# Three of five RMS-norms: four chunks' squares summed as the moving operand in four column tiles, the rest with one output column

## The chip, the cores and the metric

The kernel runs on one core of one Trainium2 chip. The metric is the device time of one execution in microseconds (us); the kernel before was run three times, and its time is the median of them.

## The reference, cut to what matters

A two-layer backbone works on a stream x of 256 tokens by 1024 channels. Each layer has a mixer (layer 0: attention beside a pooling mixer; layer 1: a Fourier mixer) and a channel mixer (layer 0: a dense SwiGLU; layer 1: a top-2-of-8 expert SwiGLU). An RMS-norm with a modulation stands ahead of each of the four, and a last norm behind them:

```python
def rmsnorm(x, g):
    x32 = x.astype(jnp.float32)
    y = x32 * lax.rsqrt(jnp.mean(x32 * x32, axis=-1, keepdims=True) + EPS)
    return (y * g.astype(jnp.float32)).astype(x.dtype)

for i in range(DEPTH):                      # DEPTH = 2
    h = modulate(x, norm_mix_g[i], sh1, sc1)    # rmsnorm(x, g) * (1 + scale) + shift
    mix_l = attention_and_pool(h) if i == 0 else fourier_mix(h)
    x = x + g1 * mix_l
    h = modulate(x, norm_ffn_g[i], sh2, sc2)
    x = x + g2 * (swiglu(h) if i == 0 else moe_swiglu(h))
return rmsnorm(x, final_g)
```

Everything is float32. What matters here is the mean of x*x over the 1024 channels of each token.

## The kernel before, in words

The stream lies transposed in SBUF: `x` is 8 chunks (KD = 8) of 128 channels by 256 tokens (T = 256). The channels of a chunk are the partitions, so a mean over channels is a sum over partitions, which TensorE does. The norms have stage numbers: 0 ahead of attention, 1 ahead of the dense SwiGLU, 2 ahead of the Fourier mixer, 3 ahead of the experts, 4 at the end. The change touches 1, 2 and 3.

The engines run in parallel, each through its own program in order; semaphores (`wait_ge`, `then_inc`) order them against one another. There is no planner: the order is written out by hand. A norm of stages 1 to 3 goes so:

- TensorE finishes output chunks in PSUM (by pairs of chunks, one bank each).
- VectorE adds each to the stream (`add_projected`, L1077; count `residual`), a chunk at a time.
- ScalarE squares each chunk of the new stream into `square_l` (`squares`, L835; count `squared`).
- TensorE averages (`mean`, L1554): for each chunk k and each half t of the tokens the squares are the *stationary* operand, 128 x 128, and a constant 128 x 128 block with 1/1024 everywhere (`C("mean")`) is the moving one. A float32 product is two pairs of instructions (LDWEIGHTS and MATMUL), so a chunk is 4 pairs and a norm 32. Every one of the 128 output columns holds the same mean; `per_token` reads column 0 of each half.
- ScalarE takes the root of 128 x 2 values (`root`, L711), VectorE the reciprocal (L1011), TensorE spreads it over the partitions (`spread_root`, L1563), and VectorE scales the stream with it.

Where `mean` stands in TensorE's order differs:

- Stage 1 (`project`, "mixout", bank 6): the last piece of the output projection is done in two halves of columns. Behind the first half (which releases residual chunks 4 and 5) stand the means of chunks 0 to 3, then the second half of columns (12 products, L1592), then chunks 4 to 7. VectorE, ahead of adding chunk 4, splits the first dense weight piece (`dense_low(0)`, L1025).
- Stage 2 (bank 2): the last dense piece goes by four pairs of output chunks (L1808, 12 products each). The means of chunks 0 and 1 stand behind pair 2 (the third), those of 2 and 3 behind pair 3 (the last), then those of 4 to 7. Behind them stand the first four products of `shift_logits` (L1849) and then `spread_root`.
- Stage 3 (`project`, "fnet", bank 0): as stage 1, but the means of 4 and 5 are followed by the first half of the router (L1895: four column tiles, the partitions 0, 32, 64 and 96 on, of a weight with 8 columns, 256 moving columns), those of 6 and 7 by its second half. Then ScalarE copies the logits (L900), TensorE turns them (L1903), VectorE picks the experts (from L1309), TensorE ranks (L1917) and gathers (L1934), and the experts begin (L1964).

`C("fold")` is a constant whose column 0 has a 1 in the partitions 0, 32, 64 and 96 and 0 elsewhere; before, it adds up the router's four tiles and those of `shift_products`. `rstd` is an SBUF tile that is unused while stages 1 to 3 run. Semaphores `cq_taken`, `kv_taken` and `shift_rows_taken` belong to the latent projections of the attention (L1137 to L1166).

Of the kernel before, what the change touches and what calls it, by code (L numbers as in the profile page):

```python
# [12 lines left out]
ACT = mybir.ActivationFunctionType  # L13
AX_X = mybir.AxisListType.X

P = 128
D = 1024
KD = D // P
T = 256
# [19 lines left out]
QUAD = 32  # L39
# [85 lines left out]
SUM_GROUPS = ((0, 2), (2, 6), (6, 10), (10, 14))  # L125
# [62 lines left out]
def build(nc, vec_d, con_d, rope_d, x_d, ctx_d, ada_d, mixa_d, mixb_d, attn_d, mixout_d, ffn_d,  # L188
          dft_d, fnet_d, router_d, moe_d, out_d):
    ctx = ExitStack()  # L190
    with ctx:
# [3 lines left out]
        def sem(name):  # L195
            return ctx.enter_context(nc.semaphore(name))
# [36 lines left out]
        def C(name):  # L233
            return con[:, CON[name][0]:CON[name][1]]
# [71 lines left out]
        def plain(ap):  # L306
# [16 lines left out]
        squared, half_squared, mean_ready, root_ready = sem("squared"), sem("half_squared"), sem("mean_ready"), sem("root_ready")  # L323
        shift_rows, shift_rows_taken, shift_ready, shift_taken, kr_gained = (
            sem("shift_rows"), sem("shift_rows_taken"), sem("shift_ready"), sem("shift_taken"), sem("kr_gained"))
        token_ready, rstd_spread = sem("token_ready"), sem("rstd_spread")
# [5 lines left out]
        mixa_ready, mixa_taken = sem("mixa_ready"), sem("mixa_taken")  # L332
        cq_taken, kv_taken = sem("cq_taken"), sem("kv_taken")
        lora_squared, lora_mean, lora_root, lora_ready = (
# [162 lines left out]
        def prep_taken(eng, n):  # L497

            s = prep_act if PREP_BY[n] == "act" else prep_dve
            eng.wait_ge(s, sum(b == PREP_BY[n] for b in PREP_BY[:n + 1]))  # L500

        PART_BANKS = (5, 6, 7, 3)
        TOK_ORDER, TOK_BANKS = (0, 2, 1, 3), (1, 3, 2, 0)
# [177 lines left out]
        def _(act):  # L681
# [78 lines left out]
            mixer_highs("mixin", 6, 8)  # L760
            act.wait_ge(shift_taken, 1)
            act.wait_ge(mixer_used, 8)
# [68 lines left out]

            def squares(need):
                for k in range(KD):
                    act.wait_ge(residual, need + k + 1)
                    nc.scalar.activation(square_l[:, k, :], x[:, k, :], ACT.Square).then_inc(squared, 1)  # L835


            nc.scalar.activation(small[:, 242:243], C("eps"), ACT.Sqrt)
            squares(0)
            root(1, per_token(6), token_root)  # L840
# [26 lines left out]
            nc.scalar.activation(small[:, 242:243], C("eps"), ACT.Sqrt)  # L867
            squares(KD)
            root(2, per_token(2), token_root)
# [18 lines left out]

            squares(2 * KD)
            root(3, per_token(0), token_root)  # L890
# [66 lines left out]
        def _(dve):  # L957
# [178 lines left out]
            dve.wait_ge(shift_rows, 1)  # L1136
            nc.vector.tensor_copy(ada_rows[:, 0:416], bank[6][:, 0:416]).then_inc(shift_rows_taken, 1)  # L1137
            dve.wait_ge(shift_ready, 1)
            nc.vector.tensor_copy(mix_shift, bank[7][:, 0:8]).then_inc(shift_taken, 1)

            dve.wait_ge(shift_taken, 1)
            dve.wait_ge(mixer_used, 8)
# [6 lines left out]
            for k in range(2):  # L1149
                ins = shifted(cqT[:, k, :], bank[3][:, k * T:(k + 1) * T], 2 * k)  # L1150
            ins.then_inc(cq_taken, 1)
            for n in range(2):
                ins = shifted(ckvT[:, n * T:(n + 1) * T], bank[4][:, n * T:(n + 1) * T], 4 + n)
            ins.then_inc(kv_taken, 1)
            dve.wait_ge(kr_ready, 1)
            dve.sem_inc(unit_free[unit_slot(first_unit["mixb"])], 1)
            for n in range(2):
                ins = shifted(krT[:, n * T:(n + 1) * T], bank[5][:, n * T:(n + 1) * T], 6 + n)
            ins.then_inc(kv_taken, 1)
            dve.wait_ge(cq_taken, 1)  # L1160
            dve.wait_ge(kv_taken, 2)
            dve.wait_ge(lora_root, 2)
# [335 lines left out]
        def _(pe):  # L1498
# [50 lines left out]
            def mean(stage, before, source, b, lo=0, hi=KD):  # L1549
# [6 lines left out]
                if hi == KD:  # L1556
                    last.then_inc(mean_ready, 1)

            def spread_root(stage, b):

                pe.wait_ge(token_ready, stage)
                for t in range(2):
                    last = mm(bank[b][:, T + t * P:T + (t + 1) * P], token_root[:, t:t + 1].to_broadcast([P, P]), C("ident"),  # L1563
                              start=(t == 0), stop=(t == 1), skip_group_check=True)
                last.then_inc(rstd_spread, 1)

            def project(name, source, banks, stage, before, b):

                for m in range(first_piece[name], first_piece[name] + len(MIXER[name])):
# [15 lines left out]
                    for columns in ((0, 1), (2, 3)) if closing else ((0, 1, 2, 3),):  # L1585
                        for left, right in PRODUCTS:
                            if left == 1:
                                pe.wait_ge(mixer_low, m + 1)
                            for j in columns:
                                c = 4 * n + j  # L1590
                                for k in range(2):
                                    last = mm(bank[banks[c // 2]][:, (c % 2) * T:(c % 2) * T + T],  # L1592
                                              parts[left][:, k, j * P:(j + 1) * P], source[right][:, k0 + k, :],
                                              start=((left, right) == PRODUCTS[0] and k0 + k == 0 and c % 2 == 0),
                                              stop=((left, right) == PRODUCTS[-1] and k0 + k == KD - 1), skip_group_check=True)
                        if closing and columns[0] == 0:
                            last.then_inc(proj_ready, 1)
                            if n == 1:
                                mean(stage, before, square_l, b, 0, 4)
                    last.then_inc(mixer_used, 1)  # L1600
                if name == "mixout":
                    mean(stage, before, square_l, b, 4)

# [57 lines left out]
            def turn_shift():  # L1661

                pe.wait_ge(shift_rows_taken, 1)
                for n in range(4):
                    last = mm(bank[7][:, 2 * n:2 * n + 2], ada_rows[:, n * P:(n + 1) * P], C("fold")[:, 0:2], start=True, stop=True)
                last.then_inc(shift_ready, 1)
# [36 lines left out]
            pe.wait_ge(attn_in, 2 * 16)  # L1703
            pe.wait_ge(kv_taken, 2)
            for n, (kind, p) in enumerate(PREP):
# [86 lines left out]
            for q, (kind, g) in enumerate(DENSE):  # L1792
# [8 lines left out]
                if q == len(DENSE) - 1:  # L1801
                    pe.wait_ge(low_ready, q + 1)
                    for pair in range(4):
# [7 lines left out]
                        last.then_inc(ffn_ready, 1)  # L1811
                        if pair >= 2:
                            mean(2, 2 + KD, square_l, 2, 2 * (pair - 2), 2 * (pair - 1))
                    continue
# [24 lines left out]
                if q in (6, 14, 22, 30):  # L1839
                    sum_up((q - 6) // 8)  # L1840
            mean(2, 2 + KD, square_l, 2, 4)
            pe.wait_ge(router_in, 16)
# [45 lines left out]
            project("fnet", fourier, FNET_BANKS, 3, 2 + 2 * KD, 0)  # L1888
            mean(3, 2 + 2 * KD, square_l, 0, 4, 6)
            for half in range(2):  # L1890
                if half == 1:
                    mean(3, 2 + 2 * KD, square_l, 0, 6)
                pe.wait_ge(h_ready, KD + 4 * half + 4)
                for c in range(4):
                    last = mm(bank[4][c * QUAD:c * QUAD + EXPERTS, 0:T], router[:, 4 * half + c, :], h[:, 4 * half + c, :],  # L1895
                              start=(half == 0), stop=(half == 1), skip_group_check=True)
# [208 lines left out]
```

## Time and profile before

| | us |
|---|---|
| median of 3 runs | 1332.42 |
| lowest and highest of them | 1331.06, 1336.16 |
| the profiled execution, its own time | 1333.01 |
| its span in the trace | 1331.1 |
| what lies around the span | 1.9 |

Mean granted TensorE clock over the profiled span: 0.997 of full speed. The time of a part is read from the starts of the instructions around it: the engine's weight loads (PEld) and products (PE) are listed apart, and a group "x16" gives the first start and the length up to the last end. An idle time in brackets stands with the engine or transfer that ended it.

### The profile page before, as it was taken

What the parts mean: (1) busy time and instruction counts of PE and PEld (TensorE: products, weight loads), DVE (VectorE), ACT (ScalarE), POOL (GpSimd) and SP (SyncE); (2) the same over time, 40 slices, a digit from 0 to 9 for tenths busy, and PEclk for the clock granted to TensorE, in tenths of its full rate; (3) what the DMA queues carried; (4) which work ended last, traced back from release to release, by engine and by line L of the source; (5) the groups of instructions that cost most, each with busy time, mean ns of one, the idle gap of its engine ahead of it and who ended that gap; (6) DMA issues with size and microseconds to landing.
All of it is one profiled execution on the core that took longest, in us unless ns stands there. A gap on an engine that the chain in (4) does not pass through costs nothing.

```text
span 1331.1 us, 28323 instructions
## 1 busy us (share of the span) xinstructions
PE 1303.4 (98%) x12611; PEld 678.6 (51%) x12611; DVE 424.2 (32%) x829; ACT 234.7 (18%) x400; POOL 16.8 (1%) x34
## 2 busy tenths in 40 slices
PE   8988999999999999999999999999999999999997
PEld 7755899999997333333333333433333333333333
DVE  5537589999765001110020020111003002011103
ACT  5156534434353000000000000010000000000002
POOL 0400000000000000000000000000000000000000
PEclk9989999999999999999999999999999999999999
DMA  9773288998735789999999999999799999999980
GB/s 381 311 299 145 96 319 344 373 367 334 288 146 203 283 359 377 409 421 360 411 420 386 406 422 395 387 399 421 309 412 420 376 404 422 421 371 411 420 361 33
DMA packets 60693, 459.97 MB, mean 346 GB/s; under 512 B 6944, under 2 KB 7200, under 8 KB 9120
## 3 DMA queue, kind: packets, MB, share of 16 engines
q1 hardware_dynamic: 60576, 458.18, 85.1%
q8 instruction: 101, 1.65, 0.5%
q14 instruction: 16, 0.13, 0.0%
HBM read 457.04 MB, written 1.11 MB: 344 GB/s over the span
## 4 chain that ended last, share of the span: by engine, by line
PE 83%; DVE 10%; DMA 4%; issue 2%; ACT 1%; SPq 0%; DVEq 0%; PEldq 0%; ACTq 0%
PE bank L1964 43%; PE bank L1977 22%; DVE work L1040 5%; DMA ring<-in_ada 4%; PE bank L1592 3%; DVE split L1025 3%; PE bank L1641 2%; PE bank L1514 2%; PE bank L1944 1%; PE bank L1554 1%; PE bank L1934 1%; PE bank L1883 1%; PE bank L1833 1%; PE bank L1766 1%; DMA ring<-in_ctx 1%
## 5 line engine op out<-in xcount | busy, mean ns | idle before, releaser
L1964 PE MATMUL bank<-ring,work 128*32 128x512 f32 (+1 forms) x6144 | 584.9, 539 | 1.1 <-DVE moe L1449 1.1
L1964 PEld LDWEIGHTS bank<-ring,work 128*32 128x32 f32 x6144 | 199.3, 110 | 377.2 <-issue 344.1
L1977 PE MATMUL bank<-ring,moe 128*32 128x512 f32 x2688 | 294.1, 592 | 0.0
L1449 DVE TENSOR_TENSOR moe<-moe,bank 128x256 f32<-128x256 f32 (+1 forms) x96 | 31.5, 383 | 658.5 <-ACT moe L929 658.5
L1977 PEld LDWEIGHTS bank<-ring,moe 128*32 128x32 f32 x2688 | 87.4, 110 | 197.6 <-issue 196.2
L929 ACT ACTIVATE moe<-bank 128x256 f32<-128x256 f32 (+1 forms) x96 | 27.4, 358 | 792.3 <-PE bank L1964 792.3
L1833 PE MATMUL bank<-split 128*128 128x256 f32 x1056 | 131.0, 284 | 1.4 <-DVE split L1025 1.2
L1833 PEld LDWEIGHTS bank<-split 128*128 128x128 f32 x1056 | 128.0, 192 | 3.5 <-DVE split L1025 1.7
L1025 DVE TENSOR_TENSOR split<-ring,split 128x2048 fp32r<-128x2048 f32 x33 | 75.5, 2290 | 11.3 <-PE bank L1592 5.9
L1040 DVE SCALAR_TENSOR_TENSOR work<-ring,condp,work 128x512 f32<-128x512 f32 x98 | 73.7, 752 | 6.3 <-DMA ring<-in_ada 2.5
L852 ACT ACTIVATE split<-ring 128x2048 fp32r<-128x2048 f32 x32 | 61.2, 1914 | 81.7 <-PE bank L1833 73.7
L1823 PE MATMUL bank<-split 128*128 128x256 f32 x480 | 59.5, 284 | 0.0
L1823 PEld LDWEIGHTS bank<-split 128*128 128x128 f32 x480 | 58.3, 192 | 0.4 <-issue 0.4
L1592 PE MATMUL bank<-split 128*128 128x256 f32 x384 | 47.2, 284 | 0.0
L1592 PEld LDWEIGHTS bank<-split 128*128 128x128 f32 x384 | 46.4, 192 | 0.4 <-issue 0.4
L1435 DVE SCALAR_TENSOR_TENSOR xT<-bank,ada,xT 128x256 f32<-128x256 f32 x64 | 25.9, 477 | 62.1 <-PE bank L1944 62.1
L973 DVE TENSOR_TENSOR split<-ring,split 128x1024 fp32r<-128x1024 f32 (+1 forms) x24 | 28.1, 1179 | 13.4 <-ACT split L702 13.3
L1453 DVE STREAM_TRANSPOSE moe<-moe 128x256 f32<-128x256 f32 (+1 forms) x96 | 31.7, 381 | 0.0
L702 ACT ACTIVATE split<-ring 128x1024 fp32r<-128x1024 f32 (+1 forms) x24 | 24.2, 1018 | 24.2 <-PE bank L1592 18.4
L1641 PE MATMUL bank<-split 128*128 128x256 f32 x168 | 24.6, 303 | 1.3 <-PE bank L1514 1.3
L1514 PE MATMUL bank<-ring,condp 128*32 128x128 f32 x640 | 21.2, 289 | 4.5 <-DMA ring<-in_ada 4.3
L1641 PEld LDWEIGHTS bank<-split 128*128 128x128 f32 x168 | 21.4, 191 | 3.5 <-issue 3.0
(233 smaller groups left out, 634.0 us busy)
## 6 DMA issues: line engine op xcount, KB each, us to landing
ring<-in_moe SPq DMA_DIRECT2D x336, 1024.0 KB, 13.5
ring<-in_ffn SPq DMA_DIRECT2D x16, 2048.0 KB, 8.8
ring<-in_ada SPq DMA_DIRECT2D x28, 1024.0 KB, 7.2
ring<-in_ada SPq DMA_DIRECT2D x10, 2048.0 KB, 10.7
ring<-in_mixout SPq DMA_DIRECT2D x2, 2048.0 KB, 10.0
ring<-in_fnet SPq DMA_DIRECT2D x2, 2048.0 KB, 9.2
ring<-in_mixa SPq DMA_DIRECT2D x2, 1024.0 KB, 17.5
tail<-tables SPq DMA_DIRECT2D x8, 256.0 KB, 17.7
```

What stands on the lines that cost most here:

```text
L852: nc.scalar.activation(high_d[:, q % SPLITS_DENSE, :], piece_view(q), ACT.Copy).then_inc(high_ready, 1)
L1025: nc.vector.tensor_tensor(low_d[:, q % SPLITS_DENSE, :], piece_view(q), plain(high_d[:, q % SPLITS_DENSE, :]), ALU.subtract).then_inc(low_ ...
L1040: ins = nc.vector.scalar_tensor_tensor(out=total, in0=half_view(h)[:, k, :], scalar=weight, in1=total, op0=ALU.mult, op1=ALU.add)
L1449: nc.vector.tensor_tensor(gate_e[:, g, 0:n], gate_e[:, g, 0:n], bank[g][:, n:2 * n], ALU.mult).then_inc(e_hidden, 1)
L1453: nc.vector.transpose(hiddenT[phase % 2][:, g, 0:n], gate_e[:, g, 0:n]).then_inc(e_turned, 1)
L1514: last = mm(bank[RUNS[run][2]][32 * j:32 * j + 32, u * P:(u + 1) * P], cond[:, k, :], w[:, k, j * P:(j + 1) * P], start=(k == 0), stop=(k ...
L1592: last = mm(bank[banks[c // 2]][:, (c % 2) * T:(c % 2) * T + T], parts[left][:, k, j * P:(j + 1) * P], source[right][:, k0 + k, :], start= ...
L1641: last = mm(out, parts[left][:, k, lo:hi], h_in[right][:, k0 + k, 0:n], start=((left, right) == PRODUCTS[0] and k0 + k == 0 and opens), st ...
L1823: last = mm(bank[FFN_BANKS[k // 2]][:, (k % 2) * T:(k % 2) * T + T], w[:, j, k * P:(k + 1) * P], hidden_parts[g % 2][:, right, j, :], star ...
L1833: last = mm(bank[kind == "w3"][:, j * T:(j + 1) * T], w[:, k, j * P:(j + 1) * P], h_parts[:, right, k, :], start=(n == 0 and j == 0 and k ...
L1964: last = mm(bank[g][c * QUAD:(c + 1) * QUAD, 0:count * P], x_group[:, 4 * half + k, j * CAP + g * QUAD:j * CAP + (g + 1) * QUAD], source[: ...
L1977: last = mm(bank[3 + n][c * QUAD:(c + 1) * QUAD, :], hiddenT[phase % 2][:, g, blk * QUAD:(blk + 1) * QUAD], source[:, j, n * 512:(n + 1) * ...
```

## The change

The means of chunks 0 to 3 become `quarters`: the constant, 32 columns of it, is the stationary operand and the squares are the moving one (256 tokens); chunk c goes to column tile c, that is, partitions 32c to 32c+31 of a bank of its own (7, 3 and 1 for stages 1, 2 and 3). ScalarE copies that bank to `rstd` between the squares of chunk 3 and of chunk 4. `mean_rest` then turns the copy to one column for each half of the tokens with `C("fold")[:, 0:1]` as moving operand, and adds the means of chunks 4 to 7 with *one* moving column in place of 128. In stage 2 all of `quarters` stands behind the last pair. Stages 0 and 4 keep theirs. Three semaphores are merged with others: `shift_rows_taken` into `shift_taken` (counts 1 and 2), `cq_taken` and `kv_taken` into `lora_taken` (3).

```diff
+        QUARTER_BANKS = (None, 7, 3, 1)
@@ ScalarE
-            def squares(need):
+            def squares(need, stage=None):
                 for k in range(KD):
+                    if stage and k == 4:
+                        act.wait_ge(quarters_ready, stage)
+                        nc.scalar.activation(rstd[:, 0:T], bank[QUARTER_BANKS[stage]][:, 0:T], ACT.Copy).then_inc(quarters_taken, 1)
                     act.wait_ge(residual, need + k + 1)
                     nc.scalar.activation(square_l[:, k, :], x[:, k, :], ACT.Square).then_inc(squared, 1)
...
-            squares(0)
+            squares(0, 1)
...
-            squares(KD)
+            squares(KD, 2)
...
-            squares(2 * KD)
+            squares(2 * KD, 3)
@@ the merged semaphores: ScalarE and VectorE, then TensorE
-            act.wait_ge(shift_taken, 1)
+            act.wait_ge(shift_taken, 2)
...
-            dve.wait_ge(cq_taken, 1)
-            dve.wait_ge(kv_taken, 2)
+            dve.wait_ge(lora_taken, 3)
...
-            pe.wait_ge(kv_taken, 2)
+            pe.wait_ge(lora_taken, 3)
@@ TensorE
+            def quarters(stage, before):
+
+                pe.wait_ge(squared, before + 4)
+                for c in range(4):
+                    last = mm(bank[QUARTER_BANKS[stage]][c * QUAD:(c + 1) * QUAD, 0:T], C("mean")[:, 0:QUAD], square_l[:, c, :],
+                              start=True, stop=True)
+                last.then_inc(quarters_ready, 1)
+
+            def mean_rest(stage, before, b, lo=4, hi=KD):
+
+                if lo == 4:
+                    pe.wait_ge(quarters_taken, stage)
+                    for t in range(2):
+                        mm(bank[b][:, t * P:t * P + 1], rstd[:, t * P:(t + 1) * P], C("fold")[:, 0:1],
+                           start=(t == 0), stop=False, skip_group_check=True)
+                for k in range(lo, hi):
+                    pe.wait_ge(squared, before + k + 1)
+                    for t in range(2):
+                        last = mm(bank[b][:, t * P:t * P + 1], square_l[:, k, t * P:(t + 1) * P], C("mean")[:, 0:1],
+                                  start=False, stop=(k == KD - 1), skip_group_check=True)
+                if hi == KD:
+                    last.then_inc(mean_ready, 1)
@@ project
                             if n == 1:
-                                mean(stage, before, square_l, b, 0, 4)
+                                quarters(stage, before)
...
                 if name == "mixout":
-                    mean(stage, before, square_l, b, 4)
+                    mean_rest(stage, before, b)
@@ the last dense piece
                         last.then_inc(ffn_ready, 1)
-                        if pair >= 2:
-                            mean(2, 2 + KD, square_l, 2, 2 * (pair - 2), 2 * (pair - 1))
+                    pe.wait_ge(ada_taken, NRUNS + len(SUM_GROUPS))
+                    quarters(2, 2 + KD)
                     continue
...
-            mean(2, 2 + KD, square_l, 2, 4)
+            mean_rest(2, 2 + KD, 2)
@@ behind project("fnet", ...)
-            mean(3, 2 + 2 * KD, square_l, 0, 4, 6)
+            mean_rest(3, 2 + 2 * KD, 0, 4, 6)
             for half in range(2):
                 if half == 1:
-                    mean(3, 2 + 2 * KD, square_l, 0, 6)
+                    mean_rest(3, 2 + 2 * KD, 0, 6)
```

## Rows read from the trace of the kernel before

**Rows 1.** The page: engines over the span.

```profile
span 1331.1 us, 28323 instructions
PE 1303.4 (98%) x12611; PEld 678.6 (51%) x12611; DVE 424.2 (32%) x829; ACT 234.7 (18%) x400; POOL 16.8 (1%) x34
```

**Rows 2.** Busy time by stretch: norm 1, dense, norm 2, norm 3, experts.

```profile
core 0: us, PE busy (x) PEld busy (x) DVE busy (x) ACT busy (x) POOL busy (x), PEclk, DMA share, GB/s
154.30:162.60 8.30, 7.73 (x58) 7.15 (x57) 5.41 (x10) 4.07 (x9) 0.00 (x0) 1.00 0.23 96
162.60:355.00 192.40, 190.99 (x1650) 187.96 (x1650) 176.92 (x192) 77.01 (x63) 0.00 (x0) 1.00 0.87 333
...
420.60:1317.00 896.40, 894.26 (x9010) 311.45 (x9009) 115.25 (x344) 43.19 (x121) 0.00 (x0) 1.00 0.93 380
```

**Rows 3.** Waits from 420.6 to 1317 us: TensorE's, then the DMA queue's.

```profile
PE bank L1964 <- DVE moe L1449: 1.1, 1, 1.1
...
SPq L547 <- PE bank L1964: 462.0, 61, 19.9
```

**Rows 4.** Timeline of norm 1: start, length, engine, line, operation, idle before.

```profile
154.33 1.88 PEld L1554 LDWEIGHTS bank<-con,ring 128*128 128x128 f32 x16
...
154.65 2.29 DVE L1025 TENSOR_TENSOR split<-ring,split 128x2048 fp32r<-128x2048 f32 x1 [5.95 <-PE bank L1592]
156.13 1.50 PEld L1592 LDWEIGHTS bank<-split 128*128 128x128 f32 x12
...
156.86 1.88 DVE L1077 SCALAR_TENSOR_TENSOR xT<-bank,ada,xT 128x256 f32<-128x256 f32 x4
157.37 0.81 ACT L835 ACTIVATE ring<-xT 128x256 f32<-128x256 f32 x2 [5.20 <-DVE xT L1077]
157.84 1.98 PEld L1554 LDWEIGHTS bank<-con,ring 128*128 128x128 f32 x16 [0.22 <-ACT ring L835]
157.84 2.17 PE L1554 MATMUL bank<-con,ring 128*128 128x128 f32 x16
158.39 0.81 ACT L835 ACTIVATE ring<-xT 128x256 f32<-128x256 f32 x2 [0.20 <-DVE xT L1077]
160.05 0.26 ACT L711 ACTIVATE small<-bank,con 128x2 f32<-128x2 f32 x1 [0.86 <-PE bank L1554]
```

**Rows 5.** Timeline of norm 2, from the means of chunks 0 and 1 on.

```profile
359.31 0.98 PEld L1554 LDWEIGHTS bank<-con,ring 128*128 128x128 f32 x8
...
360.21 1.50 PEld L1808 LDWEIGHTS bank<-split 128*128 128x128 f32 x12
...
361.63 2.77 PEld L1554 LDWEIGHTS bank<-con,ring 128*128 128x128 f32 x24
...
364.32 0.97 PEld L1849 LDWEIGHTS bank<-work,ada 128*128 128x128 f32 x8
...
365.22 0.53 PEld L1563 LDWEIGHTS bank<-con,small 128*128 128x128 f32 x4
```

**Rows 6.** Timeline of norm 3, from the means of chunks 0 to 3 on.

```profile
407.59 1.88 PEld L1554 LDWEIGHTS bank<-con,ring 128*128 128x128 f32 x16
...
409.39 1.50 PEld L1592 LDWEIGHTS bank<-split 128*128 128x128 f32 x12
...
410.81 0.98 PEld L1554 LDWEIGHTS bank<-con,ring 128*128 128x128 f32 x8
...
411.65 0.81 ACT L835 ACTIVATE ring<-xT 128x256 f32<-128x256 f32 x2 [2.41 <-DVE xT L1077]
411.92 0.12 PEld L1895 LDWEIGHTS bank<-ring,work 128*8 128x8 f32 x8
411.92 0.62 PE L1895 MATMUL bank<-ring,work 128*8 128x256 f32 x8
...
412.46 0.97 PEld L1554 LDWEIGHTS bank<-con,ring 128*128 128x128 f32 x8 [0.43 <-ACT ring L835]
...
413.55 0.12 PEld L1895 LDWEIGHTS bank<-ring,work 128*8 128x8 f32 x8
```

**Rows 7.** By line and timeline: products with two columns; the copy of 256 columns.

```profile
L1665 PE MATMUL bank<-con,ring x8: 170/251/252, 51.5 to 52.2; 128*128 128x2 f32 x8
...
51.48 0.95 PE L1665 MATMUL bank<-con,ring 128*128 128x2 f32 x8
...
L900 ACT ACTIVATE moe<-bank x1: 383/383/383, 414.3 to 414.3; 128x256 f32<-128x256 f32 x1
```

More of the change, by code:

```diff
@@ L323, in build @@
         squared, half_squared, mean_ready, root_ready = sem("squared"), sem("half_squared"), sem("mean_ready"), sem("root_ready")
-        shift_rows, shift_rows_taken, shift_ready, shift_taken, kr_gained = (
-            sem("shift_rows"), sem("shift_rows_taken"), sem("shift_ready"), sem("shift_taken"), sem("kr_gained"))
+        shift_rows, shift_ready, shift_taken, kr_gained = (
+            sem("shift_rows"), sem("shift_ready"), sem("shift_taken"), sem("kr_gained"))
+        quarters_ready, quarters_taken = sem("quarters_ready"), sem("quarters_taken")
         token_ready, rstd_spread = sem("token_ready"), sem("rstd_spread")
@@ L332, in build @@
         mixa_ready, mixa_taken = sem("mixa_ready"), sem("mixa_taken")
-        cq_taken, kv_taken = sem("cq_taken"), sem("kv_taken")
+        lora_taken = sem("lora_taken")
         lora_squared, lora_mean, lora_root, lora_ready = (
@@ L1136, in _ @@
             dve.wait_ge(shift_rows, 1)
-            nc.vector.tensor_copy(ada_rows[:, 0:416], bank[6][:, 0:416]).then_inc(shift_rows_taken, 1)
+            nc.vector.tensor_copy(ada_rows[:, 0:416], bank[6][:, 0:416]).then_inc(shift_taken, 1)
             dve.wait_ge(shift_ready, 1)
             nc.vector.tensor_copy(mix_shift, bank[7][:, 0:8]).then_inc(shift_taken, 1)
-            dve.wait_ge(shift_taken, 1)
+            dve.wait_ge(shift_taken, 2)
             dve.wait_ge(mixer_used, 8)
@@ L1150, in _ @@
                 ins = shifted(cqT[:, k, :], bank[3][:, k * T:(k + 1) * T], 2 * k)
-            ins.then_inc(cq_taken, 1)
+            ins.then_inc(lora_taken, 1)
             for n in range(2):
                 ins = shifted(ckvT[:, n * T:(n + 1) * T], bank[4][:, n * T:(n + 1) * T], 4 + n)
-            ins.then_inc(kv_taken, 1)
+            ins.then_inc(lora_taken, 1)
             dve.wait_ge(kr_ready, 1)
@@ L1158, in _ @@
                 ins = shifted(krT[:, n * T:(n + 1) * T], bank[5][:, n * T:(n + 1) * T], 6 + n)
-            ins.then_inc(kv_taken, 1)
-            dve.wait_ge(cq_taken, 1)
-            dve.wait_ge(kv_taken, 2)
+            ins.then_inc(lora_taken, 1)
+            dve.wait_ge(lora_taken, 3)
             dve.wait_ge(lora_root, 2)
@@ L1661, in turn_shift @@
             def turn_shift():
-                pe.wait_ge(shift_rows_taken, 1)
+                pe.wait_ge(shift_taken, 1)
                 for n in range(4):
```

## The prediction

> **What bounds the kernel now.** I read the page first: TensorE is busy 98% of the span, no other engine reaches a third [rows 1]. A share is an average, so next comes busy time by stretch: TensorE fills 190.99 of 192.40 us of the dense part and 894.26 of 896.40 us of the experts at full clock [rows 2]. Then the waits: through the whole expert part TensorE waits once, 1.1 us for VectorE, and never for a weight transfer; it is the DMA queue that waits for TensorE, 462.0 us in 61 waits [rows 3]. So what a norm gives back should last to the end: the parts behind it start earlier, and the loads they trigger go with them. The question is what lies on the path inside each norm, read from three timelines [rows 4 to 6]. They come out differently.
>
> **The unit prices.** A mean of one chunk is 4 pairs of load and product. Sixteen begin at 407.59 and the next kind at 409.39 [rows 6]: 1.80 us, 0.1125 a pair, 0.45 a chunk, 0.90 for two. What does a pair with *one* moving column cost? The nearest row has two columns and full-width weights: 8 products in 0.95 us, the last one 0.17 long, so (0.95 - 0.17) / 7 = 0.111 us from one to the next [rows 7]. That is the pace of 128 columns: the weight load sets it. I take 0.1125 for all pairs that stay. What shrinks is the tail of the last product: 16 products of 128 columns take 2.17 us against 1.98 for their loads [rows 4], and the difference with a load of 0.19 gives a tail near 0.26; the two-column one is 0.17 [rows 7]. That is 0.09 us a norm.
>
> On this the Trainium skill has a rule each way. "TensorE: Matmul & The Clock Gate", section "Back-to-back issue gap", gives 1 to 64 moving columns about 60 cycles and 128 columns 134, which would let the narrow products go at half the price; its section on LDWEIGHTS has the load go by its columns however few are streamed. The two-column row sides with the second. What the first would give is a rival below.
>
> The four tiles of quarters aren't in the trace; the nearest row is the router's, also four column tiles, float32, 256 moving columns: its 8 loads lie within 0.12 us, its 8 products within 0.62, and the next kind begins 0.54 after it (411.92 to 412.46) [rows 6]. Entering it costs something too: two chunks' means are worth 0.90, but from 410.81 to 411.92 is 1.11, so 0.21 of switching. Quarters thus takes 0.75 us of TensorE in place of 1.80, with bounds 0.54 (no switch) and 2.01 (tiles one after another, below), and its result is there 0.83 after its place comes up. The weights here have 32 columns, not 8, so a load may be longer; they stay hidden under products either way. The Trainium skill names the switch: "TensorEngine Tiling (Array Packing)", "Key Properties", says that a change of tiling mode drains the engine. It speaks against the change and gives no figure; with no switch the sum below would be 0.21 better in stage 3.
>
> The fold adds 4 pairs, 0.45 us. The copy is a ScalarE pass over 128 x 256 from PSUM, 0.383 us [rows 7], plus about 0.05 to be released. In pairs, a norm goes from 32 to 8 in tiles and 20 full ones; in TensorE time it saves 1.80 - 0.75 - 0.45 = 0.60 us, if nothing waits.
>
> **Stage 1: 0.09 us.** Before, VectorE is the path here: the split ahead of chunk 4 runs from 154.65 for 2.29 us, and four residual adds follow without a gap until 158.74 [rows 4]. The means of 0 to 3 and the second half of columns (12 pairs) were done in its shadow. With quarters the columns end about 1.05 us earlier, at 156.5, and the fold at 157.0, all before chunk 4 is squared at 157.78. ScalarE's copy falls into its idle 5.20 us [rows 4]. The last squares end at 159.20 as before, and 4 pairs follow. Only the tail is saved: 0.09. Of the 0.60, 0.51 is hidden; bounds: a gain of 0.2 (the 16 loads take 1.98 where the pace gives 1.88, so a little queueing) and a loss of 0.1.
>
> **Stage 2: nothing.** Before: 0.90 (means of 0 and 1) + 1.42 (last pair) + 2.69 (six chunks) lead from 359.31 to 364.32 [rows 5]. Now the last pair ends at 359.31 + 1.42 = 360.73, and quarters is ready at 360.73 + 0.83 = 361.56. But nothing is left for TensorE to do meanwhile, and ScalarE, which could have squared chunks 4 and 5 at once, stands waiting for quarters, with four squares behind the copy. The copy ends at 361.56 + 0.05 + 0.38 = 361.99. Fold: 362.05 to 362.50. The squares take 0.405 each (two in 0.81 [rows 4]): the last ends at 361.99 + 0.03 + 1.62 = 363.64. TensorE: 362.50 + 3 x 0.45 = 363.85 for the last chunk, 364.30 at its end, against 364.32. The new wait (about 0.5 us of TensorE for the copy) eats the 0.60. The tail's 0.09 is no use either: the four products of shift_logits stand ahead of the spread and end at 365.2 as before [rows 5]. I take 0; bounds: 0.3 gained (copy released faster) and 0.5 lost (copy and release slower, squares in file behind it). The added wait on ada_taken costs nothing: that sum is taken before the last piece begins.
>
> **Stage 3: 0.60 us.** Before, TensorE alone is the path: 1.80 (means 0 to 3) + 1.42 (columns) + 1.11 (4 and 5, switch) + 0.54 (router) + 1.09 (6 and 7, switch) = 5.96 us from 407.59 to the router's second half at 413.55 [rows 6]. The wait named there for ScalarE's square is none: that square ends at 412.46, as the router's first half does. Now: 0.75 + 1.42 + 0.45 + 1.11 + 0.54 + 1.09 = 5.36. Do the others keep up? Quarters is ready at 408.42, the copy at 408.85, the fold's turn comes at 409.76: there are 0.9 us of slack, which is the cover of the copy. The second half of columns ends 1.05 earlier, so chunks 6 and 7 are squared by 411.4, and their turn is at 411.86. The logits' copy, the choice of experts and the gather hang on the router in a row, so all of it moves. Bounds: 1.05 gained (fold and switch free), 0 (a wait that I don't see).
>
> The merged semaphores keep the same producer and instant each time; no cost. Final-norm and first-norm code is unchanged.
>
> **Sum:** 0.09 + 0 + 0.60 = 0.69 us. Against the profiled execution 1333.01 - 0.69 = 1332.3; it lies 0.6 above the median of the runs, so the forecast for a median is 1332.42 - 0.69 = **1331.7 us**. A measurement of this kernel can tell about 0.5%, 6.7 us, from no change; this is a tenth of that.
>
> **Rivals.**
>
> *Slower: the four quarters run one after another.* A pass of 256 columns would be twice the 0.1125 of one of 128, eight of them 1.80, with the switch 2.01 in place of 0.75. Stage 3 would go from -0.60 to +0.66. In stage 2 everything behind quarters moves by the same 1.26: +1.3. In stage 1 the slack of 0.5 to 1 takes most: +0.2. Together +2.1: 1334.5. Above about 0.60 us more per quarters stage 3 turns to a loss. Against it: the router's 8 products in 0.62 us. For it: only its narrower weights. 6%.
>
> *One moving column is cheap.* If the narrow products went at half the pace (the back-to-back rule of the Trainium skill, cited above), or at the router's, each full pair would cost about 0.03 to 0.06. Then stage 3 would be held by the squares of 6 and 7, at about 411.5: -1.7; stages 1 and 2 would lose their last chunk's wait, -0.45 each. Total -2.6: 1329.8. The two-column row is against it. 7%.
>
> *The gain in stage 3 goes nowhere.* The expert part starts earlier but finds its weights late, or the copy comes late under load. Then the sum is 0 to 0.1: 1332.3. Against it: TensorE never waits for a transfer there. 17%.
>
> *The change gives what it removes:* 1.05 us or more in each norm, -3.2: 1329.2. Stages 1 and 2 speak against it, since neither is bound there by TensorE's own work. 5%.
>
> Forecast: 62%; something not seen, either way: 3%. **Range:** the unknown terms give -1.5 to +0.6 around the median before; the runs before lie between 1331.06 and 1336.16, so a median may be off by a microsecond or two by itself. I say 1329.8 to 1334.5, which takes in the ends of two rivals. No case reaches 0.5%: same 0.94, faster 0.03, slower 0.03, both for what isn't seen.
>
> **What would show it.** Right: in norm 3 from the first quarter's load to the router's second half 5.3 to 5.5 us; 8 tile loads within some 0.15 to 0.3 us; narrow pairs at 0.11; in norm 2 a TensorE idle time of about 0.5 us released by ScalarE's copy, and shift_logits as long after the end of pair 2 as before; in norm 1 only the tail. Wrong: narrow pairs well under 0.11, quarters over 1.2 us, an expert part whose first wait is for a weight transfer, or a change of granted clock anywhere.

## The result, and the profile after

The changed kernel takes 1335.81 us (median of 20 executions, 1333.29 to 1337.32) against 1332.59 us for the kernel before (20 executions): a ratio of 1.0020, 95% interval 1.0014 to 1.0026. It is 3.2 us slower, where 0.7 us faster was forecast; the time lies above the range. The difference is within the 0.5% that the prediction named, but well outside the noise of two times 20 executions. In all that follows, one execution of e11, 1505.82 us at a granted clock of 0.845, was disturbed and is left out of that run's ratio and mean clock.

The page of the changed kernel, which answers to [rows 1]:

```profile
span 1334.5 us, 28303 instructions
PE 1306.1 (98%) x12599; PEld 679.9 (51%) x12599; DVE 425.0 (32%) x829; ACT 235.7 (18%) x403; POOL 17.5 (1%) x34
```

12 pairs fewer on TensorE, as said, and yet 2.7 us more of busy time. Busy time by stretch of the changed kernel, with the columns of [rows 2]; the number behind the POOL column is the granted clock:

```profile
154.30:162.60 8.30, 7.05 (x43) 6.41 (x42) 5.38 (x12) 5.10 (x12) 0.00 (x0) 0.79 0.08 32
162.60:355.00 192.40, 190.48 (x1650) 187.87 (x1649) 175.97 (x190) 75.98 (x61) 0.00 (x0) 1.00 0.87 332
355.00:368.00 13.00, 12.50 (x93) 11.88 (x93) 3.95 (x11) 3.48 (x10) 0.00 (x0) 0.84 0.65 275
368.00:407.60 39.60, 39.44 (x280) 37.88 (x281) 22.86 (x39) 19.99 (x39) 0.00 (x0) 0.92 0.33 133
```

The clock was 1.00 in norm 1 and the dense part before [rows 2]; now it is 0.79 in norm 1, 0.84 in norm 2 and 0.92 behind it. Finer, around norm 2 of the changed kernel:

```profile
362.00:364.00 2.00, 1.83 (x15) 1.83 (x16) 0.01 (x1) 1.33 (x5) 0.00 (x0) 0.93 0.82 344
364.00:366.00 2.00, 2.00 (x11) 2.00 (x11) 0.17 (x1) 0.26 (x1) 0.00 (x0) 0.50 0.03 8
366.00:368.00 2.00, 2.00 (x11) 2.00 (x11) 0.00 (x0) 0.00 (x0) 0.00 (x0) 0.50 0.00 0
...
372.00:374.00 2.00, 2.00 (x6) 1.60 (x5) 0.97 (x1) 2.00 (x6) 0.00 (x0) 0.51 0.00 0
374.00:376.00 2.00, 2.00 (x11) 1.73 (x10) 2.00 (x8) 1.25 (x5) 0.00 (x0) 1.00 0.00 0
```

From just under 364 to 374 us TensorE runs at 0.50, the lower of its two levels (1.2 GHz instead of 2.4), although it counts as busy all the time; 11 products fit into 2 us there where 21 did before (364 to 366, at 1.00). The timeline of the same place, which answers to [rows 5]:

```profile
355.06 5.83 PEld L1835 LDWEIGHTS bank<-split 128*128 128x128 f32 x48
...
361.03 0.64 PE L1567 MATMUL bank<-ring,con 128*32 128x256 f32 x8
...
361.73 0.38 ACT L838 ACTIVATE rstd<-bank 128x256 f32<-128x256 f32 x1 [2.14 <-PE bank L1567]
362.01 1.32 ACT L840 ACTIVATE ring<-xT 128x256 f32<-128x256 f32 x4
362.17 0.52 PEld L1576 LDWEIGHTS bank<-con,rstd 128*128 128x128 f32 x4 [0.99 <-ACT rstd L838]
...
362.61 2.52 PEld L1581 LDWEIGHTS bank<-con,ring 128*128 128x128 f32 x16
...
365.00 1.83 PEld L1876 LDWEIGHTS bank<-work,ada 128*128 128x128 f32 x8
...
365.25 0.26 ACT L713 ACTIVATE small<-bank,con 128x2 f32<-128x2 f32 x1 [1.92 <-PE bank L1581]
...
366.71 0.97 PEld L1590 LDWEIGHTS bank<-con,small 128*128 128x128 f32 x4
...
369.61 8.95 PEld L1895 LDWEIGHTS bank<-ring 128*128 128x128 f32 x32 [0.22 <-issue]
```

Up to the fold everything stands where the prediction put it: quarters in 0.64, the copy 0.38, TensorE's wait for the copy. Then the narrow run slows down within itself (16 loads in 2.52 us, which should be 1.88), and what stands behind takes twice as long: the products of shift_logits 1.83 instead of 0.97 [rows 5].

In norm 1 the fall comes behind the root. TensorE and ScalarE of the changed kernel:

```profile
156.66 1.86 PEld L1581 LDWEIGHTS bank<-con,ring 128*128 128x128 f32 x16 [0.78 <-ACT ring L840]
...
158.64 0.26 ACT L713 ACTIVATE small<-bank,con 128x2 f32<-128x2 f32 x1 [0.86 <-PE bank L1581]
...
159.16 1.22 PE L1590 MATMUL bank<-con,small 128*128 128x128 f32 x4 [0.55 <-DVE small L1016]
159.96 2.77 PEld L1538 LDWEIGHTS bank<-con 128*128 128x128 f32 x8
```

Norm 3 went as forecast and a little better (compare [rows 6]):

```profile
411.95 0.16 PEld L1567 LDWEIGHTS bank<-ring,con 128*32 128x32 f32 x8
...
412.52 1.49 PEld L1619 LDWEIGHTS bank<-split 128*128 128x128 f32 x12 [0.41 <-issue]
...
413.94 0.53 PEld L1576 LDWEIGHTS bank<-con,rstd 128*128 128x128 f32 x4
...
414.39 0.97 PEld L1581 LDWEIGHTS bank<-con,ring 128*128 128x128 f32 x8
...
415.38 0.12 PEld L1922 LDWEIGHTS bank<-ring,work 128*8 128x8 f32 x8
...
415.93 0.97 PEld L1581 LDWEIGHTS bank<-con,ring 128*128 128x128 f32 x8 [0.43 <-ACT ring L840]
...
416.91 0.12 PEld L1922 LDWEIGHTS bank<-ring,work 128*8 128x8 f32 x8
```

The 3.4 us between the two spans can be laid out by milestones that both traces have: the root of each norm (ScalarE), the first residual addition of norm 2 (VectorE), the first row product of the Fourier mixer, the first expert load. Each number is the difference of two starts.

| stretch, us (root 1 means the root of norm 1, and so on) | before | after | difference |
|---|---|---|---|
| start to root 1 | 160.05 | 158.64 | -1.41 |
| root 1 to first addition of norm 2 (dense) | 196.77 | 198.27 | +1.50 |
| first addition to root 2 | 7.81 | 8.34 | +0.53 |
| root 2 to the Fourier row products | 9.79 | 13.34 | +3.55 |
| those to root 3 | 39.24 | 38.43 | -0.81 |
| root 3 to the first expert load | 12.89 | 12.90 | +0.01 |
| expert load to the end | 904.55 | 904.58 | +0.03 |

So 4.1 us are lost in and behind norm 2. Norm 1 and the dense part about cancel. Of the -1.41, 1.18 comes ahead of the norm, where the code does the same (VectorE's split starts at 153.47 instead of 154.65 [rows 4]). The trace of the kernel before has a low stretch of its own there, behind a wait of TensorE for a transfer. The same 64 products start at 81.14 us before and at 81.12 after; the products at 90.25 before are those at 89.07 after, 1.18 us sooner. Around them the clock is at 0.50 for 6.8 us before (from just under 80 us on) and for 3.4 us after. The stretches from 84 to 88 us of the kernel before:

```profile
84.00:86.00 2.00, 1.67 (x17) 0.81 (x10) 0.69 (x1) 0.00 (x0) 0.00 (x0) 0.50 1.02 434
86.00:88.00 2.00, 2.00 (x5) 0.91 (x4) 0.00 (x0) 0.72 (x2) 0.00 (x0) 0.83 0.97 418
```

And of the changed kernel:

```profile
84.00:86.00 2.00, 1.66 (x19) 0.77 (x8) 0.69 (x1) 0.16 (x1) 0.00 (x0) 1.00 1.00 426
86.00:88.00 2.00, 2.00 (x6) 0.76 (x4) 0.00 (x0) 1.48 (x3) 0.00 (x0) 1.00 0.99 426
```

Two theories for the low clock: **N**, the narrow products (one moving column) keep TensorE listed as busy but stream almost nothing; **W**, the new wait for the copy, or the change of tiling, lets it idle.

### The profile page after: what moved, and what is told of

Same layout as the page of the kernel before. It is cut to its first block, busy times and chain, and to the rows that moved or that the text cites. A ratio compares the mean times of both kernels' runs of the same rounds, so it can differ in the third digit from the quotient of the medians.

```text
span 1334.5 us, 28303 instructions
## 1 busy us (share of the span) xinstructions
PE 1306.1 (98%) x12599; PEld 679.9 (51%) x12599; DVE 425.0 (32%) x829; ACT 235.7 (18%) x403; POOL 17.5 (1%) x34
## 4 chain that ended last, share of the span: by engine, by line
PE 82%; DVE 11%; DMA 3%; issue 2%; ACT 1%; SPq 0%; DVEq 0%; PEldq 0%; ACTq 0%
PE bank L1991 43%; PE bank L2004 22%; DVE work L1045 5%; PE bank L1619 3%; DVE split L1030 3%; DMA ring<-in_ada 3%; PE bank L1668 2%; PE bank L1518 2%; PE bank L1971 1%; PE bank L1961 1%; PE bank L1910 1%; PE bank L1895 1%; PE bank L1860 1%; PE bank L1793 1%; PE bank L1786 1%
```

## The experiments

Every kernel below was executed 9 to 12 times. "Before" is the kernel before on the same chip. "Clock" is the mean over all executions of a kernel of its granted clock over the span: 0.997 for the kernel before in every group (single executions 0.994 to 0.998), 0.992 for the change (0.991 to 0.993). The two ranges don't touch. "The root-2 stretch" is the table's row from root 2 to the Fourier row products, 9.79 us before.

**e1: quarters, but wide products.** The separation of the two theories.

```diff
-                        last = mm(bank[b][:, t * P:t * P + 1], square_l[:, k, t * P:(t + 1) * P], C("mean")[:, 0:1],
+                        last = mm(bank[b][:, t * P:(t + 1) * P], square_l[:, k, t * P:(t + 1) * P], C("mean"),
```

> The change with one thing put back: in all three norms the means of chunks 4 to 7 stream 128 columns again instead of 1; quarters, copy, fold and every wait stay. Theory N (narrow products leave TensorE's array nearly idle, and the granted clock falls to 0.5 behind norm 1 and norm 2): the clock stays at 1.0 through both norms and the 40 us behind them, the dense-to-Fourier stretch loses its 3 to 4 us, and the time is 0.5 to 1.2 us under the kernel before (about 1331.7). Theory W (it is the new wait for ScalarE's copy, or the change of tiling, that lets the clock fall): both are still there, so the clock falls as in the changed kernel and the time stays about 3 us above before.

Measured: 1331.88 us against 1332.63, ratio 0.9994 (0.9985 to 1.0004); clock 0.997. Weight loads of e1 around norm 2:

```profile
361.58 0.52 PEld L1576 LDWEIGHTS bank<-con,rstd 128*128 128x128 f32 x4 [0.99 <-ACT rstd L838]
362.02 1.87 PEld L1581 LDWEIGHTS bank<-con,ring 128*128 128x128 f32 x16
363.81 0.97 PEld L1876 LDWEIGHTS bank<-work,ada 128*128 128x128 f32 x8
```

Its clock from 364 to 366 us, where the change has 0.50:

```profile
364.00:366.00 2.00, 2.00 (x21) 2.00 (x19) 0.71 (x3) 0.26 (x1) 0.00 (x0) 1.00 0.03 8
```

The wait (0.99 in both), the copy, the tiling and the fold are there; only the streamed columns differ, and the clock stays. W falls as the cause of the change's falls. The loads of 128-column products take 1.87 us, the pace forecast for one column: narrowing had bought no pace. Norm 3 of e1, from its weight loads:

```profile
407.28 0.16 PEld L1567 LDWEIGHTS bank<-ring,con 128*32 128x32 f32 x8
...
410.82 0.12 PEld L1922 LDWEIGHTS bank<-ring,work 128*8 128x8 f32 x8
...
412.45 0.12 PEld L1922 LDWEIGHTS bank<-ring,work 128*8 128x8 f32 x8
```

Its stretch from the Fourier row products to root 3 is 38.65 us, 0.59 under before.

**e2: the kernel before, with narrow products for chunks 4 to 7.** The other half of the change alone.

```diff
+                        w = 1 if k >= 4 and stage != 4 else P
-                        last = mm(bank[b][:, t * P:(t + 1) * P], source[:, k, t * P:(t + 1) * P], C("mean"),
+                        last = mm(bank[b][:, t * P:t * P + w], source[:, k, t * P:(t + 1) * P], C("mean")[:, 0:w],
```

> The kernel before with one thing added: in the same three norms the means of chunks 4 to 7 stream 1 column instead of 128; no quarters, no copy, no fold, no new wait. Theory N: the granted clock falls to 0.5 behind norm 1 or norm 2 or both, and the time is 2 to 4 us above before. Theory W: the clock is that of the kernel before, and the time is 0 to 0.3 us under it (shorter tails).

Measured: 1334.75 us against 1332.63, ratio 1.0012 (1.0003 to 1.0021); clock 0.9935. Its weight loads around norm 2:

```profile
362.11 2.77 PEld L1555 LDWEIGHTS bank<-con,ring 128*128 128x128 f32 x24
364.79 1.18 PEld L1850 LDWEIGHTS bank<-work,ada 128*128 128x128 f32 x8
...
366.70 1.83 PEld L1850 LDWEIGHTS bank<-work,ada 128*128 128x128 f32 x8
```

No quarters and no copy, and the clock falls all the same, some 2.5 us after the narrow run began (24 loads are 8 wide and 16 narrow ones), against 1.1 us in the change. The root-2 stretch is 12.35 us, 2.56 more than before, against 3.55 more in the change. N holds. The rest of the 3.55 does not need both parts of the change: e5 below, whose norm 2 is that of the change, has 12.34 us, and e11, which has no quarters, 13.75. What differs between these traces is how long the low stretch lasted (the table behind e12).

**e3: quarters in norm 3 alone**, wide products, norms 1 and 2 as before.

```diff
-            squares(0, 1)
+            squares(0)
-            squares(KD, 2)
+            squares(KD)
-                                quarters(stage, before)
+                                quarters(stage, before) if name == "fnet" else mean(stage, before, square_l, b, 0, 4)
```

> Quarters, copy and fold in the third norm alone, its remaining means 128 columns wide; norms 1 and 2 are those of the kernel before. Both theories on the clock expect none of it to fall. By the sum of the prediction, corrected by the trace of the changed kernel (from the first quarter's load to the router's second half 5.2 us instead of 5.96): 0.6 to 0.8 us under before, all of it made in the third norm and kept through the experts. If the gain is lost behind the norm the time is that of before within 0.2 us.

Measured: 1331.99 us against 1332.63, ratio 0.9998 (0.9989 to 1.0007); clock 0.9967. The stretch from the Fourier row products to root 3 is again 38.65 us, so the 0.59 is quarters' own, in norm 3. But this trace holds a fall that was not expected: 0.66 and 0.50 from 366 to 370 us, behind a norm 2 that is the one of the kernel before, costing 1.49 us (11.28 instead of 9.79). So the kernel before stands close to this edge itself. The expectation that none of the clock falls here was a miss.

**e4: narrow products, with filler in front.** Two 256-column products ahead of the fold in norms 1 and 2.

```diff
                 if lo == 4:
+                    if stage < 3:
+                        keep_warm(2, 3 if stage == 1 else 0)
                     pe.wait_ge(quarters_taken, stage)
```

> The change, narrow products kept, with two 256-column products (4 instructions, about 0.86 us) into an idle bank ahead of the fold in norms 1 and 2, in TensorE's wait. Theory N in its strict form (the narrow run itself of 16 pairs, 1.8 us, is what lets the clock fall): it still falls behind norm 2, perhaps not behind norm 1, and the time is 1 to 3 us above before. Theory W (the idle time in front is what counts): the clock stays, and the time is within 0.7 us of before.

Measured: 1334.79 us against 1332.63, ratio 1.0020 (1.0010 to 1.0031); clock 0.9924. Work ahead of the narrow run did not prevent the fall: the root-2 stretch is still 12.82 us. The filler was a little longer than the wait (7.98 us from the first addition to root 2, against 7.80 in e1). This agrees with N in its strict form, though the fall comes 2.3 us after the end of the narrow run here, not within it.

**e5 and e6: where it costs.** 128 columns in norm 1 alone, and in norm 2 alone.

```diff
+                        w = P if stage == 1 else 1      # e5
+                        w = P if stage == 2 else 1      # e6
```

> The change with 128 columns put back in norm 1 alone; norms 2 and 3 keep one column. If each norm's own narrow run lets the clock fall behind it: the clock is 1.0 behind norm 1 and falls to 0.5 behind norm 2; mean clock over the runs about 0.994; time 1.5 to 3 us above before, since the low stretch behind norm 2 was the long one (8 to 10 us against 3). If norm 1 alone is to blame the time is that of e1, 0.7 us under before.

> The change with 128 columns put back in norm 2 alone; norms 1 and 3 keep one column. If each norm's own narrow run lets the clock fall behind it: about 3 us at 0.5 behind norm 1, 1.0 behind norm 2; mean clock about 0.995; time within 1 us of before, since behind norm 1 TensorE waits for ScalarE anyway and much of the low stretch is filler. If norm 2 alone is to blame, time and clock of e1.

e5: 1334.78 us against 1332.34, ratio 1.0016 (1.0007 to 1.0024), clock 0.9937. e6: 1332.18 against 1332.34, ratio 1.0002 (0.9993 to 1.0011), clock 0.9943. Each norm's narrow run is followed by its own fall: the trace of e5 has 1.00 around norm 1 and a root-2 stretch of 12.34 us; that of e6 has 0.50 around norm 1 and a root-2 stretch of 9.78. Norm 2 is the one that costs: e6 lies within 1 us of the kernel before, as expected, and e5 2.4 us above it. Both traces show something new: a fall behind norm 3, which had none in the traces of the change, e2 and e4, with the same narrow products. Root 3 to the first expert load is 13.83 and 13.82 us there instead of 12.89.

**e7: 64 columns in all three norms.**

```diff
+                        w = 64
```

> The change with 64 columns in the means of chunks 4 to 7 of all three norms: weight loads, pace and all waits as in the change, half the array work of the kernel before. If it is the streamed columns that count, and gradually, the clock falls behind fewer of the runs or for a shorter time than with one column (mean clock 0.994 to 0.996, time 0 to 2 us above before). If only the number of products counted, it would be that of e1; if only a full 128 columns hold it, that of the change (0.992, 3 us above).

Measured: 1333.12 us against 1332.34, ratio 1.0011 (1.0002 to 1.0021); clock 0.9947, single executions from 0.992 to 0.997. With 1, 64 and 128 columns the clocks are 0.992, 0.995 and 0.997, at the same number of products, the same loads and the same waits. The effect is graded: the streamed columns count. (These three were not all timed on one chip; the kernel before has 0.997 in each group.)

**e8: narrow in norm 3 alone.**

```diff
+                        w = 1 if stage == 3 else P
```

> The change with 128 columns in norms 1 and 2 and one column in norm 3 alone, where no low clock was seen behind it in any trace so far. Expected: no fall of the clock but those of the kernel before, mean clock 0.997, and the time 0.7 to 1.0 us under before: quarters' 0.6 in norm 3 and 0.2 more, since behind a narrow run the switch to the router's tiles came 0.10 us sooner, twice. If a fall appears behind norm 3 as well, the time is at or above before.

Measured: 1332.72 us against 1332.34, ratio 1.0004 (0.9995 to 1.0013); clock 0.9955. The expected gain is a miss. Around norm 3 of e8 by stretch:

```profile
412.00:414.00 2.00, 2.00 (x19) 1.49 (x18) 0.17 (x1) 0.73 (x3) 0.00 (x0) 0.76 0.39 49
414.00:416.00 2.00, 2.00 (x11) 2.00 (x11) 1.19 (x7) 1.12 (x2) 0.00 (x0) 0.50 0.86 356
416.00:418.00 2.00, 1.85 (x11) 1.54 (x10) 1.73 (x11) 1.82 (x4) 0.00 (x0) 0.89 1.03 422
```

The clock falls here too; the norm ends 0.2 us sooner with narrow products (38.45 against 38.65) and loses 0.95 behind it. Norm 3 is not immune: of the eight traces with narrow products there, three have a fall behind it (e5, e6, e8) and the change, e2, e4, e7 and e11 have none. This trace has a fall behind its wide norm 2 as well, as in e3.

**e9: e1 once more**, to settle whether it beats the kernel before; the same kernel.

> The kernel of e1 once more (quarters, fold and copy in three norms, 128 columns in the means of chunks 4 to 7), to settle whether it beats the kernel before. If the sum of the prediction holds once the clock is left alone: mean clock 0.997, median 0.4 to 1.0 us under before, as in e1 (0.75 under). If e1 was luck: within 0.2 us of before.

Measured: 1332.94 us against 1332.41, ratio 1.0005 (0.9996 to 1.0015); clock 0.9964. The 0.75 of e1 did not repeat. Together e1 and e9 have a mean of 1332.65 us over 23 executions, the kernel before 1332.74 over 62 on the same two chips. With a standard deviation of 1.5 us from one execution to the next, 23 of them can't settle a gain of 0.6.

**e10: e1 with filler in norm 2's wait.**

```diff
+                    if stage == 2:
+                        keep_warm(1, 0)
                     pe.wait_ge(quarters_taken, stage)
```

> e1 with one 256-column product (2 instructions, 0.43 us) into an idle bank in norm 2, in TensorE's idle half microsecond ahead of the fold. Behind norm 2 the clock also fell in two traces whose norm 2 was 128 columns wide (e3, e8), so a fuller stretch there may spare some of these: mean clock 0.997 to 0.998, time 0 to 0.5 us under e1. If the filler delays the fold (it is meant to fit into the wait) the time is 0.1 to 0.3 us over e1 and the clock the same.

Measured: 1332.25 us against 1332.41, ratio 0.9998 (0.9988 to 1.0008); clock 0.9969. The filler fits into the wait (first addition to root 2: 7.80 us, as in e1) and changes nothing that can be measured.

**e11: all eight chunks narrow**, without quarters: the suspected cost doubled.

```diff
+                        w = 1 if stage != 4 else P
```

> The suspected cost doubled: the kernel before with one moving column in the means of all eight chunks of norms 1 to 3 (32 pairs each, not 16). No quarters, no copy. If the narrow products are the cause: the clock falls behind all three norms or stays low longer than in e2 (mean clock 0.993 there), mean clock 0.989 to 0.992, time 3 to 6 us above before, over e2's 2.1. If the clock depends on the last pairs ahead of the spread alone, as in e2: 0.993 and 2 us.

Measured: 1335.31 us against 1332.41, ratio 1.0019 (1.0010 to 1.0028); clock 0.9927. The time lies 2.9 us above before, just under the expected 3 to 6, and the clock just above the expected 0.989 to 0.992. The root-2 stretch is 13.75 us against 12.35. The ratio's interval overlaps that of e2 (1.0012, 1.0003 to 1.0021), so more narrow pairs are not shown to cost more; twice as many don't double the loss. That the first chunks' products are interleaved with wide ones may be why; no run shows it.

**e12: e1 with wider products behind norm 2.** The products of shift_logits stream 64 columns instead of 8.

```diff
-                    last = mm(bank[7][:, 0:EXPERTS], ada[:, at:at + 1].to_broadcast([P, P]), router[:, k, :],
+                    last = mm(bank[7][:, 64 - 8 * k:128 - 8 * k], ada[:, at:at + 1].to_broadcast([P, P]), work[:, 3456:3520],
```

> e1 (quarters in three norms, 128 columns in the rest) with the eight products of shift_logits behind norm 2 streaming all 64 router columns instead of 8, their own eight landing at columns 64 to 71 of the bank. The pace stays that of the weight load, so their time should not change by itself. If streamed columns hold the clock, the falls that remained behind norm 2 with 128-column means (seen in the traces of e3 and e8, 1.5 us each) become rarer: mean clock 0.9975 or more against 0.9968 for e1 and e9 together, time 0 to 0.5 us under them. If those falls have another cause: clock 0.997 and the time of e1 and e9, 1332.7.

Measured: 1331.66 us against 1331.87, ratio 0.9997 (0.9988 to 1.0006); clock 0.9975, but 0.9973 for the kernel before on that chip. Eight times the columns cost nothing: their 8 loads take 0.97 us as before. Whether they spare falls behind norm 2 isn't told apart by this run.

**All traces together.** How long the clock stayed low behind norm 2 adds up from the granted clock of stretches of 2 us. It sorts the traces:

| low for, us | traces | columns in norm 2's means of chunks 4 to 7 | root-2 stretch, us |
|---|---|---|---|
| 0 | before, e1, e6, e9, e10, e12 | 128 | 9.78 to 9.79 |
| 3.4 | e3, e8 | 128 | 11.28 |
| 6.8 | e2, e4, e5, e7 | 1 (e7: 64) | 12.3 to 12.8 |
| 10.2 | the change, e11 | 1 | 13.34, 13.75 |

All six traces with fewer than 128 columns there have a fall, and two of the eight with 128, both shorter.

No version beats the kernel before by what can be measured. The 57 executions of kernels with quarters and wide products (e1, e9, e10 and e12, and e3 with quarters in norm 3 alone) lie 0.35 us under the kernel before on the same chips, in a mean weighted by chip, with a standard error of 0.20. That rules out neither a gain of nothing nor the 0.69 forecast.

## Why the prediction was wrong

**Bound and propagation: right.** What norm 3 gives back lasts to the end: the experts take 904.55 us before, 904.58 after, and between 904.54 and 904.65 in all fourteen traces. The one wait of TensorE there is unchanged:

```profile
PE bank L1991 <- DVE moe L1453: 1.1, 1, 1.1
```

**Unit prices in TensorE's time: right.** Quarters' 8 loads within 0.16 us and 8 products within 0.64; narrow pairs at the pace of the weight load. By line, the narrow products of the changed kernel, first column minimum, median and maximum in ns:

```profile
L1581 PEld LDWEIGHTS bank<-con,ring x48: 186/192/333, 156.7 to 416.7; 128*128 128x128 f32 x48
L1581 PE MATMUL bank<-con,ring x48: 250/250/352, 156.7 to 416.7; 128*128 128x1 f32 x48
```

A load is 192 ns as before. Between the two rules of "TensorE: Matmul & The Clock Gate" in the Trainium skill this case's trace decides for the weight load, and the rival of the cheap column has no support; nor has that of quarters running one after another.

**Stage 3: right, 0.60 forecast.** 0.59 in e1 and e3, and 0.81 with narrow products. The sign named for it was off: from the first quarter's load to the router's second half it is 5.17 us in e1 (407.28 to 412.45) and 4.96 in the change, not 5.3 to 5.5. The prediction counted the 0.21 of switching inside this stretch, but it falls ahead of that first load: 0.79 is saved inside the stretch in e1 and 0.59 between the milestones, and 5.36 less 0.21 is 5.15. The extra 0.2 is from the switch into the router's tiles: the two-chunk run and the switch take 0.99 us (414.39 to 415.38) where they take 1.10 in e1 (409.72 to 410.82), twice.

**Stage 2: the order of events was right, the result wrong.** Nothing gained was forecast, and e1 shows just that: 7.80 us from the first addition to root 2 against 7.81 before, with TensorE's half microsecond of waiting where it was said to be. In the change it is +0.53 and then +3.55, with the clock at 0.50 from 363.7 to 374 us; e1, which keeps the clock, has neither.

**Stage 1: a tail of 0.09 was forecast, and it is lost in something larger.** From VectorE's split to root 1 it takes 5.40 us before, 5.28 in e1 and 5.17 in the change: 0.11 for the tail and 0.12 from quarters, both within the bounds. From root 1 to VectorE's scaling it took 1.27 us before (160.05 to 161.32) and 1.77 after (158.64 to 160.41), since the spread runs at half the clock. That half microsecond is the cost of the fall there, when it comes ahead of the spread (in e4 and e6 it comes later, and this stretch is as long as before); the filler behind it, 2.77 us instead of 1.60, is hidden by ScalarE's passes.

**The step that failed** is the price of a narrow pair, in one sentence of the unit prices: "I take 0.1125 for all pairs that stay." It priced a narrow pair by the time TensorE spends on it and took the clock for a constant, because it was 1.00 in every row read. "A change of granted clock anywhere" stood among the things that would prove the forecast wrong, but had no price and no chance in it. The term left out is +4.1 us in norm 2 and +0.5 in norm 1 by the trace; against it stood a forecast gain of 0.69. What low clock costs could have been read in the trace of before: 64 products with 32-column weights take 3.64 us at 81.14, at 0.50, and 1.95 at 71.03, at 1.00. That narrow products bring it about could not be read there; the runs e1, e2 and e7 showed it. The Trainium skill, "TensorE: Matmul & The Clock Gate", "Part 1: The HAM clock gate", has the clock follow how busy TensorE has been. These runs agree, with this to add, that a product which the profile lists as busy may count for little (2.00 of 2.00 us busy at 0.50, behind the narrow run of the change).

**What stays open.** The dense part took 196.2 to 198.4 us in fourteen traces, longest in some with a fall behind norm 1 (198.27, 198.38) and in one without (198.30), so its +1.50 here isn't shown to be the change's. Only 0.23 of it arises by 178 us (one of VectorE's splits starts at 178.45 before and at 177.27 after); the rest comes later, at a clock of 1.00 in both. What makes a fall last 3.4, 6.8 or 10.2 us, and come within a narrow run or 2.3 us behind it, is open. And how often the kernel before itself falls behind norm 2 was not counted; its own trace has none, the traces of e3 and e8, wide in norm 2, one each. But its spread goes with its clock: of 112 executions 46 have a clock of 0.998 and a mean of 1331.67 us, 38 have 0.997 and 1332.83, 19 have 0.996 and 1333.23, and nine have 0.995 or less and 1334.36.

## What to carry to other kernels

A product whose pace is set by its weight load gains next to nothing from fewer moving columns (here 0.11 us for the last product's tail and 0.11 at a switch of tiles), and it can lose the clock for what comes after. Where such a run stands ahead of a serial stretch, leave the columns wide, even if only one is read, and read the granted clock by stretches of 2 us in every comparison. The busy share won't tell. One trace of each version isn't enough either: the same norm had falls of different lengths, or none, from one trace to the next, so take the mean clock over many executions beside it.

## What the runs showed of the hardware that was not expected

With everything else equal, the mean granted clock over a 1332 us span was 0.992, 0.995 and 0.997 for 1, 64 and 128 moving columns in 48 pairs. Those pairs take some 5.4 us together. In the trace of the change the clock fell within a run of 20 such pairs (fold included; norm 2) or just behind it (norm 1) and came back after 10 us and 3 us, while the profile showed TensorE fully busy at both levels in norm 2 (2.00 of 2.00 us). Two full-width products of 256 moving columns right before such a run did not prevent the fall (e4).
